# Moving the operand buffer by 9408 bytes and reordering the matmuls of one feed-forward product

## What is computed

```python
# first block (h is an RMS norm of x, weighted)
proj = h @ w_in                       # attention and recurrence inputs
x = x + mix @ w_out
mq = hq @ w_mq;  mk, mv = split(mk @ w_mkv)
x = x + m_o @ w_mo
u = causal_dwconv(hf @ w_up, conv_w, conv_b)      # 2048 -> 11264   "up"
a, b = split(u)
x = x + (silu(a) * b) @ w_down                    # 5632 -> 2048    "down"
x = rmsnorm(x, final_norm_w)
# second block
u = h @ w_in_2                        # conformer, pooling and gated parts
y = concat(...) @ w_out_2
x = x + rms_norm(y, norm_mix_post)
up = causal_depthwise_conv(h @ w_up_2, conv_w) + conv_b    # "up_2"
gate, val = split(up)
f = (silu(gate) * val) @ w_down_2                 # "down_2"
x = x + rms_norm(f, norm_ffn_post)
```

## Time and profile before

| | us |
|---|---|
| median of three runs | 2654.44 |
| lowest, highest | 2654.02, 2654.53 |
| span of the profiled execution | 2652.2 |
| PE busy | 2642.4 (100% of the span) |
| PEld busy | 2332.9 (88%) |
| DVE busy | 1789.4 (67%) |
| ACT busy | 1345.5 (51%) |
| POOL busy | 150.3 (6%) |

### The profile page before, as it was taken

One profiled execution on the slowest core, in us unless ns is written; L12 is line 12 of the kernel. 1 busy time (PEld: TensorE's weight loads), 2 busy tenths in 40 slices (PEclk: granted clock), 3 DMA queues, 4 the chain that ended last, 5 costly groups with the idle time before them and its releaser, 6 DMA issues.

```text
span 2652.2 us, 41690 instructions
## 1 busy us (share of the span) xinstructions
PE 2642.4 (100%) x15689; PEld 2332.9 (88%) x15689; DVE 1789.4 (67%) x2188; ACT 1345.5 (51%) x1647; POOL 150.3 (6%) x106
## 2 busy tenths in 40 slices
PE   9999999999999999999999999999999999999999
PEld 9888898889999888888888889998888888888887
DVE  7677567565645777777775456998777777776444
ACT  6554375464533655555553344444665555554443
POOL 2001200000200200000001222000020000000000
PEclk9999999999999999999999999999999999999999
DMA  8655456546545566566666665655566656656564
GB/s 260 192 160 187 139 182 185 178 154 203 177 129 167 184 192 189 188 188 188 188 189 191 190 190 173 196 187 174 168 191 190 190 189 187 187 188 206 191 192 148
DMA packets 256256, 487.12 MB, mean 184 GB/s; under 512 B 15069, under 2 KB 80629, under 8 KB 255616
## 3 DMA queue, kind: packets, MB, share of 16 engines
q1 hardware_dynamic: 254496, 476.11, 57.1%
q0 software_dynamic: 1488, 9.19, 1.0%
q10 hardware_dynamic: 144, 0.01, 0.0%
HBM read 483.12 MB, written 2.13 MB: 183 GB/s over the span
## 4 chain that ended last, share of the span: by engine, by line
PE 94%; DVE 4%; ACT 1%; POOL 1%; issue 0%; DVEq 0%; ACTq 0%; POOLq 0%
PE ps L2107 94%; DVE w_lo L1325 1%; DVE acc L1854 1%; POOL sumsq L724 1%; ACT w_hi L784 0%; DVE ya L1918 0%; DVE x_res L2088 0%; DVE ua L1359 0%; ACT lnz L1219 0%; PE ps L2640 0%; PE ps L2427 0%; DVE y_lo L1390 0%; DVE ya L1920 0%; DVE cvp L1908 0%; DVE ya L1914 0%
## 5 line engine op out<-in xcount | busy, mean ns | idle before, releaser
L1325 DVE TENSOR_TENSOR w_lo<-raw,w_hi 128x1024 fp32r<-128x1024 f32 x899 | 1119.2, 1247 | 785.6 <-ACT w_hi L784 784.4
L2107 PE MATMUL ps<-op,w_hi 128*128 128x512 f32 (+1 forms) x6208 | 1638.8, 353 | 0.1
L784 ACT ACTIVATE w_hi<-raw 128x1024 fp32r<-128x1024 f32 x899 | 949.4, 1059 | 1106.3 <-PE ps L2107 1088.2
L2107 PEld LDWEIGHTS ps<-op,w_lo 128*128 128x128 f32 x5024 | 948.4, 189 | 170.4
L2107 PE MATMUL ps<-op,w_lo 128*128 128x256 f32 x5024 | 1089.5, 279 | 0.0
L2107 PEld LDWEIGHTS ps<-op,w_hi 128*128 128x128 f32 x6208 | 955.2, 190 | 4.2 <-issue 1.8
L2107 PE MATMUL ps<-g,w_hi 128*128 128x512 f32 x704 | 219.6, 393 | 0.0
L2107 PE MATMUL ps<-w_hi,g 128*128 128x512 f32 x704 | 217.7, 390 | 0.0
L2107 PE MATMUL ps<-w_hi,op 128*128 128x512 f32 x512 | 163.5, 393 | 0.0
L2107 PEld LDWEIGHTS ps<-w_hi,g 128*128 128x128 f32 x704 | 132.1, 188 | 30.2
L2107 PEld LDWEIGHTS ps<-g,w_lo 128*128 128x128 f32 x704 | 132.4, 188 | 30.0
(11 more groups left out here) (318 smaller groups left out, 1534.6 us busy)
## 6 DMA issues: line engine op xcount, KB each, us to landing
raw<-in_weights SPq DMA_DIRECT2D x899, 512.0 KB, 4.5
x_res<-in_x SPq DMA_DIRECT2D x8, 256.0 KB, 5.6
mem_x<-in_mem POOLq DMA_DIRECT2D x1, 2048.0 KB, 8.8
x_res<-in_x POOLq DMA_DIRECT2D x1, 2048.0 KB, 9.9
w_row<-row_dram POOLq DMA_DIRECT2D x2, 1024.0 KB, 7.8
out_x<-x_res SPq DMA_DIRECT2D x3, 512.0 KB, 2.9
rel_rev<-rel_dram POOLq DMA_DIRECT2D x1, 1024.0 KB, 8.3
hg_con<-in_hg_consts POOLq DMA_DIRECT2D x1, 576.0 KB, 5.2
```

What stands on the lines that cost most here:

```text
L784: nc.scalar.activation(w_hi[:, s], raw[:, s], ACT.Copy).then_inc(hi_rounded, 1)
L1325: TT(w_lo[:, s], raw[:, s], w_hi[:, s].bitcast(F32), ALU.subtract).then_inc(chunk_split, 1)
L2107: return nc.tensor.matmul(out, lhsT, rhs, start=start, stop=stop, skip_group_check=True)
```

## The change

`op` is placed behind the parameters, constants and statistics instead of ahead of them. These take 9408 bytes, so that `op` begins at 91456. The parameters and statistics move down by 32768 bytes, the size of `op`. The arena, `x_res` and the weight buffers stay where they are. In `up_2` the sequence of the sixteen matmuls of a chunk is `ROWS_TOGETHER`; in `up` it stays `TWO_TILES`.

```diff
         x_at = at[0]
         x = place("x_res", [P, KT, TOK])
-        op_at = at[0]
-        op = place("op", [P, KT, 2, TOK], F32R)
-        op_hi, op_lo = op[:, :, 0], op[:, :, 1]
         par = place("par", [P, NPAR])
         con = place("con", [P, NCON])
...
         rstd = place("rstd", [P, 2, TOK])
         ones_r = place("ones_r", [P, P], F32R)
+        op_at = at[0]
+        op = place("op", [P, KT, 2, TOK], F32R)
+        op_hi, op_lo = op[:, :, 0], op[:, :, 1]
         arena = at[0]
...
-            product_halves(GM["up_2"], op, halves("up_2"), beside_up_2(), 4, TWO_TILES)
+            product_halves(GM["up_2"], op, halves("up_2"), beside_up_2(), 4, ROWS_TOGETHER)
```

## The result

The changed kernel takes 2635.2 us (median of five, 2635.13 to 2635.72) against 2654.28 us beside it (median of five, 2653.87 to 2654.53). The ratio is 0.9929, 95% interval 0.9918 to 0.9940: faster by 0.71%, 19.1 us. The prediction said 2651.9 us with a range from 2644.5 to 2664.5.

A forecast was written before the change was run, and what follows sets the result against it. The prediction took the kernel to be bound by PE, by the distances between matmul starts. Its terms were -2.5 us for up_2 and 0 for all else, so 2654.44 - 2.5 = 2651.9 us, range 2644.5 to 2664.5.

The forecast's parts named there:

- What bounds the kernel: Whole kernel: PE is busy 2642.4 of 2652.2 us; only distances between matmul starts can change, a few ns each.
- part 5: All else, such as other engines' writes to `op` and moved parameters: 0, ±0.5 us.
- Part 1: up_2's 176 chunks get down's order and place, 14.3 ns less each: -2.5 us, bounds 0 and -5.0 us.
- Part 2: 304 two-tile chunks of up and the Q parts, order kept, place new: 0, bounds -4.3 and +10.7 us.
- Rival A: Place alone makes down fast, for every order; all 480 two-tile chunks gain 6.8 us: 2647.6 us or lower; chance 0.26.
- Part 3: 64 token-major chunks with `op` stationary: taken as 0, upper bound +1.7 us at 2.2 ns a matmul.
- Part 4: 148 single chunks, 3552 matmuls at 120.0 ns: taken as 0, far bounds -17.8 and +7.8 us.
- Rival B: The new place clashes, hidden in down by order; up, Q parts and token-major lose: net +9.9 us, 2664.3 us; chance 0.20.
- Rival C: Nothing moves; down's speed comes from what runs beside it, such as a less busy DVE: 2654.4 us; chance 0.06.

The follow-up runs named there:

- e1: The changed kernel with up_2 put back to TWO_TILES, so that only the buffer is moved: 2634.57 us, ratio 0.9929 to the kernel before.
- e2: The kernel before with up_2 alone in ROWS_TOGETHER, the buffer not moved: 2653.90 us, ratio 1.0001 to the kernel before.
- e8: The changed kernel with the arena 832 bytes later, so that g and y_hi move: 2634.19 us, ratio 0.9927 to the kernel before.
- e13: The changed kernel with the arena 64 bytes later, `op` left where it was: 2634.23 us, ratio 0.9924 to the kernel before.
- e15: The changed kernel itself, run and profiled once more: 2634.98 us, ratio 0.9927 to the kernel before.
- e14: The changed kernel without the four fp32 matmuls of pool_mix in gated: 2636.07 us, ratio 0.9933 to the kernel before.
- e5: The kernel before with every buffer 64 bytes later, weights included, all distances between buffers kept: 2653.70 us, ratio 1.0001 to the kernel before.

## Why the prediction was wrong, step by step

**What bounds the kernel: right.** The time is in the main the sum of distances between matmuls; PE's busy time fell by 21.2 us and the span by 18.8; that 2.4 us of it went into waits is dealt with under part 5.

**Part 1 (up_2, -2.5 us): right in size, wrong in cause.** Measured -2.2 us in the window of 164 chunks. e1 and e2 show that the order has no part. I had kept order and place together because up_2 got both; e2 alone would have parted them.

**Part 2 (up and the Q parts, 0, bound -4.3 us): the lower bound was nearly the truth.** up's window fell by 2.2 us, 13 ns a chunk, which would be 4.0 us on 304 chunks. Rival A had these chunks right, and I gave it 0.26. The reason for 0, that one order at the new place has about the distances of the other order at the old one "within 0.5%", was none, since 0.5% was the very difference to be explained.

**Part 3 (token-major, 0, bound +1.7 us): the upper bound was nearly the truth.** hg_i has 228.9 instead of 226.8 ns, and all three stages together lose 1.3 us in the trace. It was the place and not the order (e8, e13).

**Part 4 (single chunks, 0): this step failed, and it is the largest term.** The sentence was "24 of 24 matmuls at 120.0 ns look like a limit that knows no addresses". The changed profile has 113.3 and 117.8 ns, and 113.3 for somewhat more than half of them. With 3552 such matmuls the distances add up to -15.9 us in the first profile. How much it is hangs on the share of the two rhythms: in e15's it is -17.0 us, in e1's -18.0. The far bound, -17.8 us, had been written down from the 115 ns of the earlier trace rows, but rival A has of it only the words "lower still", and it did not enter the range. I had explained the short distance away ("the loading of stationary operands can catch up; with 256 columns throughout it can't") without a row for it. The regularity of 120.0 ns was that of one distance between the buffers and not that of a floor.

**Part 5 (all else, 0 ± 0.5 us): nearly right.** 1.4 us were given back in out_2, where the prediction had named the conformer taps as leading and not asked what a faster TensorE does there.

**Rival B** had the sign of the token-major stages right and its spread to the two-tile form wrong. Its sign is not wrong for the place as such: at 96, 160 or 224 bytes a move makes the kernel 10 to 18 us slower. **Rival C** fell with e1 and with up's window.

In sum, by the distances from start to start over the whole of both traces: -6.0 us for the 480 two-tile chunks, +1.3 for token-major with `op`, -15.9 for single chunks, -0.6 for all other matmuls, and 2.4 us of new idle time of PE. That is the measured -18.8 us. The main error is one term, part 4, put at 0; without it the result would have lain inside the range.

## What to carry to other kernels

Where TensorE never waits, place is a tuning parameter: in this kernel the distance between the buffers that it reads at once was worth up to 7 ns a matmul, and it costs nothing to change. Scan it in steps of 32 bytes up to 256, and for each form of matmul apart, since what is best for one is not best for another. A distance that is constant to the last digit isn't thereby a floor; put it into the sum at the shortest that the trace shows for that size, and carry that bound into the range. And ask of every stage that gets faster which engine is next: in out_2 it was VectorE at once, and in e14 a fall of the clock followed the longer wait.

## What the runs showed of the hardware

The start-to-start time of matmuls with float32 operands (in the fp32r form) at 2.4 GHz depends on the distance, by 256 bytes, between the place of the stationary and that of the moving operand: 113.6 to 120.2 ns in the table's windows with 256 columns, 226.8 to 234.2 ns with 512 (token-major), and 2761 to 2828 ns for a chunk of eight of each. Only the difference counts (e5, for 64 bytes), and the two orders of tile and row cost the same (e1 against the changed kernel, e2 against the kernel before).

At one distance there can be two steady rhythms (113.3 and 117.8 ns), and other matmuls in between can switch from one to the other (e14). Why a distance costs time was not seen: the traces give starts and not reads, and no run separates a bank of the memory from a buffer of the engine.

After a wait of 2.85 us (e14) and one of 1.95 us (e13) the granted clock fell to its lower level for some 3 us, after one of 2.0 us (e8) it did not.

The Trainium skill's page "SBUF — State Buffer" (section "Who interferes with whom") says that PE's two read ports are independent and that it waits for nobody. If its two reads were independent in every respect, the distance between them would not matter; in these runs it does: with `op` moved by 64 bytes, and beside it only the small buffers (e3), the kernel is 0.58% faster.
